# The low parts of two weight chunks behind each norm, on VectorE instead of GpSimd and ahead of the sum of token tile 1

## What is computed

```python
x = _layer_norm(DEEPNORM_ALPHA * x + mix, ln1_g[layer], ln1_b[layer])
ffn = _swiglu(x, ffn_w_gate[layer], ffn_w_up[layer], ffn_w_down[layer])
x = _layer_norm(DEEPNORM_ALPHA * x + ffn, ln2_g[layer], ln2_b[layer])
```

## Time and profile before

| | |
|---|---|
| median of three runs | 1008.08 us (1004.07 to 1009.12) |
| span of the profiled execution | 1007.4 us |
| PE busy | 969.2 us, 96% |
| DVE busy | 591.3 us, 59% |
| ACT busy | 490.5 us, 49% |
| POOL busy | 45.7 us, 5%, of it 23.0 in the eight subtractions |
| granted TensorE clock, mean | 0.983 of full |

### The profile page before, as it was taken

One profiled execution on the slowest core, in us unless ns is written; L12 is line 12 of the kernel. 1 busy time (PEld: TensorE's weight loads), 2 busy tenths in 40 slices (PEclk: granted clock), 3 DMA queues, 4 the chain that ended last, 5 costly groups with the idle time before them and its releaser, 6 DMA issues.

```text
span 1007.4 us, 13625 instructions
## 1 busy us (share of the span) xinstructions
PE 969.2 (96%) x4630; PEld 798.9 (79%) x4630; DVE 591.3 (59%) x976; ACT 490.5 (49%) x789; POOL 45.7 (5%) x38
## 2 busy tenths in 40 slices
PE   7999989999999899999899999997999999999997
PEld 5888867888888688887678888885888888888875
DVE  3786677555544743455865555448455666564664
ACT  4775544444443363355354444344555654654433
POOL 1100024000000200000200000002000000000000
PEclk9999999999999998999999999999999999999999
DMA  8743337666566262243266566562655455355551
GB/s 290 251 168 105 108 109 259 223 187 188 174 197 188 72 221 90 90 122 122 86 230 188 186 177 192 186 197 80 230 189 170 123 188 167 126 168 180 197 187 63
DMA packets 46371, 168.10 MB, mean 167 GB/s; under 512 B 5256, under 2 KB 5400, under 8 KB 45680
## 3 DMA queue, kind: packets, MB, share of 16 engines
q1 hardware_dynamic: 44064, 156.09, 48.5%
q0 software_dynamic: 2256, 11.32, 3.1%
HBM read 166.35 MB, written 1.05 MB: 166 GB/s over the span
## 4 chain that ended last, share of the span: by engine, by line
PE 88%; DVE 8%; ACT 2%; issue 1%; DMA 1%; DVEq 0%; SPq 0%; ACTq 0%
PE psum L497 20%; PE psum L503 19%; PE psum L500 19%; PE psum L545 17%; PE psum L677 3%; DVE w_lo L1112 3%; PE psum L649 3%; PE psum L663 1%; PE psum L634 1%; PE psum L465 1%; DVE x L1280 1%; PE psum L598 1%; DVE x L1256 1%; DVE x L1264 1%; DVE ln_st L1245 1%; PE psum L683 1%
## 5 line engine op out<-in xcount | busy, mean ns | idle before, releaser
L1112 DVE TENSOR_TENSOR w_lo<-stage,w_hi 128x1024 fp32r<-128x1024 f32 (+2 forms) x291 | 364.0, 1262 | 200.1 <-ACT w_hi L823 196.4
L823 ACT CAST w_hi<-stage 128x1024 fp32r<-128x1024 f32 (+2 forms) x299 | 304.8, 1035 | 145.1 <-PE psum L503 76.6
L497 PE MATMUL psum<-w_hi,xt_hi 128*128 128x512 f32 (+3 forms) x816 | 327.7, 402 | 3.2 <-ACT w_hi L823 2.1
L500 PE MATMUL psum<-w_lo,xt_hi 128*128 128x512 f32 (+3 forms) x816 | 319.8, 392 | 11.4 <-DVE w_lo L1112 11.4
L503 PE MATMUL psum<-w_hi,xt_lo 128*128 128x512 f32 (+3 forms) x816 | 319.6, 392 | 1.2 <-DVE xt_lo L1147 0.9
L500 PEld LDWEIGHTS psum<-w_lo,xt_hi 128*128 128x128 f32 x816 | 157.4, 193 | 43.4 <-DVE w_lo L1112 16.3
L497 PEld LDWEIGHTS psum<-w_hi,xt_hi 128*128 128x128 f32 x816 | 157.2, 193 | 36.5 <-issue 5.9
L503 PEld LDWEIGHTS psum<-w_hi,xt_lo 128*128 128x128 f32 x816 | 156.9, 192 | 32.7 <-DVE xt_lo L1152 1.9
L545 PE MATMUL psum<-w_hi,ht_hi 128*128 128x512 f32 x224 | 71.2, 394 | 1.0 <-ACT ln_par L1072 0.7
L545 PE MATMUL psum<-w_lo,ht_hi 128*128 128x512 f32 x224 | 70.2, 390 | 0.0
L545 PE MATMUL psum<-w_hi,ht_lo 128*128 128x512 f32 x224 | 70.2, 389 | 0.0
(11 more groups left out here) (143 smaller groups left out, 833.6 us busy)
## 6 DMA issues: line engine op xcount, KB each, us to landing
stage<-in_w_up SPq DMA_DIRECT2D x88, 512.0 KB, 3.7
stage<-in_w_down SPq DMA_DIRECT2D x44, 512.0 KB, 3.8
stage<-in_w_cd_in SPq DMA_DIRECT2D x28, 440.0 KB, 3.3
stage<-in_w_in_a SPq DMA_DIRECT2D x24, 512.0 KB, 4.4
stage<-in_w_in_b SPq DMA_DIRECT2D x16, 512.0 KB, 3.7
stage<-in_w_ab_in SPq DMA_DIRECT2D x12, 480.0 KB, 6.5
ln_par<-in_ln POOLq DMA_DIRECT2D x4, 1024.0 KB, 6.3
stage<-in_w_ab_out SPq DMA_DIRECT2D x8, 512.0 KB, 3.5
```

What stands on the lines that cost most here:

```text
L497: pe.matmul(acc, ah, wh, start=(k == 0), stop=False)
L500: pe.matmul(acc, ah, wl, start=False, stop=False)
L823: act.copy(w_hi[:, s, 0:w], stage[:, s, 0:w]).then_inc(hi_done, 1)
L1112: dve.tensor_tensor(w_lo[:, s, 0:w], stage[:, s, 0:w], w_hi[:, s, 0:w].bitcast(F32), ALU.subtract).then_inc(lo_done, 1)
```

## The change

GpSimd loses `split_two`, its count `pool_lo` and the map `POOL_CHUNKS`. `chunk_lo` is plain `lo_done` for every chunk. DVE computes the low parts of the third and fourth chunk itself: `split_to(done["chunks"] + 2)` stands behind `turn_and_split` and ahead of the sum of tile 1 at all four norms (at norm 3 behind the reciprocal of `second_root(0)`), and `join_pool` is gone. The load of `cum` moves behind the wait for x of norm 0.

```diff
-AFTER_NORM = ("up0", "cd_in", "up1", "in_a")
-POOL_CHUNKS = {GEMMS[name].c0 + 2 + m: 2 * n + m + 1 for n, name in enumerate(AFTER_NORM) for m in range(2)}
...
-            return (pool_lo, POOL_CHUNKS[c]) if c in POOL_CHUNKS else (lo_done, c + 1)
+            return lo_done, c + 1
...
-            def split_two(name):
-
-                for c in (GEMMS[name].c0 + 2, GEMMS[name].c0 + 3):
-                    s, w = c % NS, WIDTH[c]
-                    pool.wait_ge(hi_done, c + 1)
-                    pool.tensor_tensor(w_lo[:, s, 0:w], stage[:, s, 0:w], w_hi[:, s, 0:w].bitcast(F32), ALU.subtract
-                                       ).then_inc(pool_lo, 1)
-
-            split_two(AFTER_NORM[0])
             pool.wait_ge(head_done, STREAMS["l0"][1])
...
-            load("cum", cum_tri, d["cum"])
             for k in range(1, 4):
                 pool.wait_ge(x_ready, 2 * TT * k)
+                if k == 1:
+                    load("cum", cum_tri, d["cum"])
                 load(f"ln{k}", ln_par[:, :, :].rearrange("p a n -> p (a n)"),
                      bass.AP(tensor=d["ln"].tensor, offset=2 * D * k, ap=[[0, P], [1, 2 * D]]))
-                split_two(AFTER_NORM[k])
...
                 turn_and_split(name)
+                split_to(done["chunks"] + 2)
                 sum_tile(k, projection, 1)
                 norm_tile(k, 1)
                 turn(name, xt_hi, xt_lo, 0, [1])
-                join_pool()
...
             second_root(0)
+            split_to(done["chunks"] + 2)
             sum_tile(3, "down1", 1)
...
             second_root(1)
-            join_pool()
```

More of the change, by code:

```diff
@@ L212, in build_program @@
         hi_done, lo_done = sem("hi_done"), sem("lo_done")
-        pool_lo = sem("pool_lo")
         chunk_used = sem("chunk_used")
@@ L1287, in turn_and_split @@
                     turn_part(part, xt_hi, xt_lo, 0, name)
[L1289 to L1294, removed]
             def norm_and_turn(k, projection, name):
```

## The result

The changed kernel takes 1007.73 us (median of 20 runs, 1003.69 to 1008.88), the kernel before 1004.35 us (median of 20, 1003.27 to 1009.12). The ratio is 1.0021, 95% interval 1.0011 to 1.0031: 2.1 us slower, which is inside the 0.5% that I called the same. The two medians lie further apart, 3.4 us, because the runs of both kernels come in groups: eleven of the twenty before lie under 1004.5, three of the twenty after. The sum in the prediction was +1.7 us; its absolute time, 1009.8, stood on the median of the first three runs, which lay high among the twenty.

The account below looks back on a forecast made before the run. The prediction took PE's own pace to bound most of the span, with DVE holding the end at the four norms. Its norm terms, together +1.7 us, were added to the median 1008.08: 1009.8 us, range 1006.5 to 1012.5.

Parts of the forecast that it names:

- The sum: Norm 0 +3.0, norm 1 -0.35, norm 2 -1.4, norm 3 +0.5 us; together +1.7 us.
- GpSimd and DVE exclude each other at a port: At the norms one engine holds the port; freeing DVE gains 1.4, 1.1, 1.4 and 0.9 us at norms 0 to 3.
- The table work moves forward into norm 0: At norm 0 GpSimd's position-bias table work comes at 139.6 instead of 158.21 and delays DVE by 5.0 us.
- the length of the hold: At norm 0 the wide table operation holds the port 3.95 us, the first, half as wide, 2.0.
- The clock: PE idles about 3.5 us ahead of tile 1, then slow products cost 1.4 us, at norms 1 and 3.
- The wait at 364.58: PE's 0.65 us wait for a low part whose chunk was late goes, as SP loads earlier; counted at norm 1.
- The base of the sum: The sum was added to the median of the kernel before, 1008.08 us (1004.07 to 1009.12), giving 1009.8.
- table work that misses the norm: Rival, 20%: the table work doesn't delay DVE at norm 0, which gains 2.0 instead of losing 3.0; 1004.8 us.
- a port held for all of GpSimd's record: Rival, 4%: the two table records hold the port 8.5 us, norm 0 loses 3.5 more; 1013.3 us.
- a DVE that isn't freed: Rival, 2%: low parts stay near 3 us for another reason, each norm about 4 us longer; 1024 us.
- A clock that stays low for longer: Rival, 14%: slow products in tile 1 cost a further 1.5 us at all four norms; 1015.8 us.

Follow-up runs that it names:

- experiment 3: The changed kernel with unread PE products added ahead of tile 1's transposes, table work where the change puts it; ratio 0.9982 to the kernel before.

## Why the prediction was right or wrong

- **GpSimd and DVE exclude each other at a port** was right, and so was the count: low parts of 1.22 us (1.07 at norm 1, with 880 columns), but for the one behind the table work, and from the first one to the sum 5.13 (5.2 forecast), 5.73 (5.8) and 6.66 us (6.8) at norms 1 to 3.
- **The table work moves forward into norm 0** was right: forecast for 139.6, there at 139.93, its load 8.96 us behind the issue. The term for it in the sum was mis-sized, 5.0 us where 3.64 was measured (0.8 and 2.8). The step that failed is the length of the hold. I had counted the wide operation's hold from its start at 161.06, but the low part at 160.35 had the port until 161.58. From there to the blocked part's turn at 165.0 are 3.4 us, not 3.95. And the narrow one held 0.75, not the half of the wide one that I had put at 2.0: the unhindered low part at 160.35, which I took to agree with 2.0, agrees with 0.75 as well.
- **The clock** was right in kind: PE idle 3.18, 3.02 and 2.26 us ahead of tile 1 at norms 1 to 3, slow products behind it, gone when the idle time is filled. In size, norms 1 to 3 of the changed kernel lost 2.2, 2.4 and 0.7 us against experiment 3, where I had charged 1.4 at norm 1, nothing new at norm 2 and 1.4 at norm 3. At norms 1 and 2 about 0.35 us of it is in the transposes behind the wait, which I had not priced.
- **The wait at 364.58** is gone: PE has no wait on a low part in that stretch.
- **The sum**: +3.0, -0.35, -1.4, +0.5 forecast, and in the table +1.4, +1.0, -0.7, -0.3 for the two profiled executions (the 0.65 us at norm 1 lie outside of it). The total, +1.7, stands beside 2.1 by the ratio over 20 runs each, and 3.4 between the medians. That it comes so near owes something to luck: norm 0 was forecast too high and norm 1 too low.
- **The base of the sum** is the step that failed in the stated time. The sum was added to 1008.08, the median of three runs between 1004.07 and 1009.12. Over twenty runs the kernel before has 1004.35, 3.7 us less. So 1009.8 is 5.5 us above the kernel before, where the ratio makes the change 2.1; from 1004.35 the same sum gives 1006.0, 1.7 under the measured 1007.73. I had also set the span of 1007.4 beside the median and found it 0.7 under; the whole of that execution is about 1009.1, 1.0 over it. What made it slow is at least in part the stretch between norms 1 and 2, where its clock was granted at 0.72 from 396 to 406 with no gap in PE's records. That the same stretch separates the kernel's quick runs from its slow ones is likely but not shown, since only one of its executions has a trace.
- **The rivals**: table work that misses the norm is out by the trace; a port held for all of GpSimd's record is out by the low part of 4.05 us, which would have waited until 149.19 and taken 5.9; a DVE that isn't freed is out by the low parts. A clock that stays low for longer happened in part, at norms 1 and 2.

## What to carry to other kernels

When work leaves a queue, look at what stood behind it there: here the position-bias work moved 18 us forward, into the one place where DVE was what everybody waited for, and one wait in front of it gave back 3.6 us on DVE. When a supplier gets faster, look at where the consumer will now stand idle. Here PE idled for 3.18 us at norm 1 and then ran at a granted clock of 0.50; unread products in the gap, once it is in one piece, together with that wait turned a change that lost 0.2% into one that gains 0.7%. When an engine is held up by another, work out when it got its turn, and not only when the other's record ends. And take the level of a kernel from more than three runs before adding a sum to it.

## What the runs showed of the hardware

- A VectorE subtraction or norm with both inputs in SBUF waits for a GpSimd operation that reads SBUF (2.8 and 3.2 us behind one of 2048 elements a partition) and not for one that writes (1.22 us beside five memsets). GpSimd waits in the same way: the wide operation is on record for 5.2 us from when it has the port, and for 5.89 and 6.31 where a low part had it first.
- GpSimd's multiplication holds the port for 0.75 us with 1024 elements a partition and 3.35 with 2048. VectorE got its turn 1.87 to 1.94 us before the end of GpSimd's record at both widths.
- PE's clock also fell where its records leave no gap: 0.72 granted in the kernel before from 396 to 406, with PE busy 10.00 of 10 us. What brings it about there is open.
- The 24 products of tile 1 at norms 0 and 2 took from 5.7 to 8.1 us, by where the slow stretch fell.
